# Modulation of a transformer block pair: matmul strips replaced by VectorE dot products over a transposed weight, and the first context-key product moved behind the branch products

## What is computed

```
mod     = silu(c)     @ w_mod + b_mod   -> shift1, scale1, gate1, shift2, scale2, gate2
mod_ctx = silu(c_ctx) @ w_mod + b_mod   -> shift1, scale1 (only these two are used)
h   = rmsnorm(x)   * (1 + scale1) + shift1          attention input of block 2
ctx = rmsnorm(ctx) * (1 + scale1_ctx) + shift1_ctx  its context keys and values
x   = x + gate1 * attention(h, [ctx, h])
h2  = rmsnorm(x) * (1 + scale2) + shift2            input of router and experts
x   = x + gate2 * experts(h2)
```

## Time and profile before

| | value |
|---|---|
| median of 3 runs | 1057.99 us (1057.42 to 1058.18) |
| span of the profiled execution | 1055.0 us |
| what lies around the span, median less span | 3.0 us |
| PE busy | 988.6 us, 94% |
| DVE busy | 525.0 us, 50% |
| ACT busy | 423.2 us, 40% |
| POOL busy | 154.5 us, 15% |
| DMA | 246.60 MB, mean 234 GB/s |

### The profile page before, as it was taken

The page is one execution under the profiler, slowest core; times in us unless marked ns, Lnnn a source line. Parts: engine busy times, 40 slices in busy tenths (PEclk is TensorE's granted clock), DMA queues, the critical chain, the costliest instruction groups (busy, mean ns, idle before and its releaser), DMA issues.

```text
span 1055.0 us, 13905 instructions
## 1 busy us (share of the span) xinstructions
PE 988.6 (94%) x5609; PEld 733.3 (70%) x5609; DVE 525.0 (50%) x703; ACT 423.2 (40%) x619; POOL 154.5 (15%) x97
## 2 busy tenths in 40 slices
PE   5999999888999999999999989999999999999992
PEld 5997888665998988988798856666776444344331
DVE  5656654783665445546607516777466222212224
ACT  4446844523454334435444434565232322222111
POOL 4001000000000000000097844455000000000000
PEclk9999999988999999999999999999997999999997
DMA  9745552439644764757354522325898899999981
GB/s 306 249 146 199 199 185 95 160 123 332 221 162 160 271 235 148 264 180 255 124 169 152 182 98 80 116 85 188 319 356 331 330 421 421 422 421 421 421 362 42
DMA packets 84675, 246.60 MB, mean 234 GB/s; under 512 B 4420, under 2 KB 8283, under 8 KB 72191
## 3 DMA queue, kind: packets, MB, share of 16 engines
q1 hardware_dynamic: 82224, 240.20, 60.9%
q0 software_dynamic: 1408, 4.00, 1.4%
q10 hardware_dynamic: 974, 1.45, 0.4%
HBM read 244.59 MB, written 1.05 MB: 233 GB/s over the span
## 4 chain that ended last, share of the span: by engine, by line
PE 83%; DVE 10%; ACT 2%; issue 2%; DMA 2%; POOL 1%; SPq 0%; DVEq 0%; POOLq 0%; ACTq 0%
PE gemm_ps L1268 10%; PE gemm_ps L774 8%; PE gemm_ps L776 8%; PE gemm_ps L775 8%; PE gemm_ps L778 7%; PE gemm_ps L780 7%; PE gemm_ps L779 7%; PE gemm_ps L1309 6%; PE gemm_ps L959 2%; PE mix_ps L774 2%; PE mix_ps L775 2%; PE mix_ps L776 2%; DVE w_lo L457 2%; PE mix_ps L1319 1%; PE mix_ps L1074 1%
## 5 line engine op out<-in xcount | busy, mean ns | idle before, releaser
L451 ACT ACTIVATE w_hi<-ring 128x1024 fp32r<-128x1024 f32 (+2 forms) x222 | 227.2, 1035 | 237.1 <-PE gemm_ps L780 95.0
L457 DVE TENSOR_TENSOR w_lo<-ring,w_hi 128x1024 fp32r<-128x1024 f32 (+2 forms) x174 | 203.7, 1187 | 164.2 <-ACT w_hi L451 163.4
L778 PE MATMUL gemm_ps<-acts,w_hi 128*128 128x256 f32 x640 | 184.9, 289 | 4.1 <-DVE acts L1851 2.8
L774 PE MATMUL gemm_ps<-w_hi,acts 128*128 128x512 f32 (+2 forms) x448 | 176.6, 394 | 8.0 <-DVE w_lo L457 7.1
L779 PE MATMUL gemm_ps<-acts,w_hi 128*128 128x256 f32 x640 | 181.8, 284 | 0.0
L780 PE MATMUL gemm_ps<-acts,w_lo 128*128 128x256 f32 x640 | 181.8, 284 | 0.0
L775 PE MATMUL gemm_ps<-w_lo,acts 128*128 128x512 f32 (+2 forms) x448 | 171.9, 384 | 0.0
L776 PE MATMUL gemm_ps<-w_hi,acts 128*128 128x512 f32 (+2 forms) x448 | 171.7, 383 | 0.0
L457 POOL TENSOR_TENSOR w_lo<-ring,w_hi 128x1024 fp32r<-128x1024 f32 x48 | 122.6, 2573 | 89.1 <-ACT w_hi L451 89.1
L778 PEld LDWEIGHTS gemm_ps<-acts,w_hi 128*128 128x128 f32 x640 | 123.5, 193 | 9.5 <-issue 6.2
L779 PEld LDWEIGHTS gemm_ps<-acts,w_hi 128*128 128x128 f32 x640 | 123.5, 193 | 1.3 <-issue 1.2
(11 more groups left out here) (367 smaller groups left out, 1317.3 us busy)
## 6 DMA issues: line engine op xcount, KB each, us to landing
ring<-in_w_in_dram SPq DMA_DIRECT2D x56, 1024.0 KB, 5.0
ring<-in_w_mod_dram SPq DMA_DIRECT2D x24, 1024.0 KB, 5.7
ring<-in_w_ffn_in_dram SPq DMA_DIRECT2D x20, 1024.0 KB, 5.1
late_ring<-in_w_exp_down_dram SPq DMA_DIRECT2D x20, 1024.0 KB, 16.8
late_ring<-in_w_exp_gate_dram SPq DMA_DIRECT2D x18, 1024.0 KB, 15.7
late_ring<-in_w_exp_up_dram SPq DMA_DIRECT2D x18, 1024.0 KB, 14.0
ring<-in_w_ffn_out_dram SPq DMA_DIRECT2D x11, 1024.0 KB, 9.2
ring<-in_w_exp_up_dram SPq DMA_DIRECT2D x9, 1024.0 KB, 17.3
```

The lines of the kernel that those rows point to most:

```text
L451: nc.scalar.activation(part(w_hi, u), raw_unit(u), ACT.Copy).then_inc(hi_made, 1)
L457: eng.tensor_tensor(part(w_lo, u), raw_unit(u), part(w_hi, u), ALU.subtract).then_inc(lo_made[unit["maker"]], 1)
L774: mm(dst, xh, wh, start=a_, stop=False, skip_group_check=True)
L778: mm(dst, wh, xh, start=a_, stop=False, skip_group_check=True)
```

## The change

The host hands over `w_mod` transposed (6144 x 1024), so that a feature's weights lie along a row. Each of 32 loads brings 256 features (1 MB, two rows of 1024 for each partition) through the same ring. DVE multiplies each row with SiLU of `c` or `c_ctx`, which lies on all partitions (`c_rows`, two DMAs on POOL's queue and two ACT operations), sums it and adds the bias, with one `tensor_tensor_reduce` for 128 features; `mod_dots(n)` does n loads. The context's parts come first and are read separately from those of `c`, so 32 MB of `w_mod` are loaded where it was 24 MB. The loads lie in the ring at 13 places among the gate chunks, 4 around `w_out`, and 15 in the feed-forward, none later. The gates' columns are multiplied into diagonals by POOL (`gate_diagonal`) and spread by one product with ones (`gate_spread`). All strips, turns and bias products of the modulation, and their copies on ACT, are gone.

The context rows are now scaled on ACT, turned in the middle of the branch products, and converted on ACT alone (`half_cols`) with DVE's subtraction (`half_low`) between the branch adds. On PE the first context-key chunk follows the branches directly, with the turn of the merged rows in its middle, then both halves of `w_out`, then the second context-key chunk. The merged rows are converted straight from PSUM in two halves (`high_cols`, `low_cols`). The sides of `acts` (0 and 1) are exchanged for the operands, and the slots of the expert weights are filled in another order: those in the ring as soon as their last piece is split.

```diff
+MODS = [("ctx", part, j) for part in (0, 1) for j in range(0, KT, 2)]
+MODS += [("c", part, j) for part in (0, 1, 3, 4) for j in range(0, KT, 2)]
+MODS += [("gate", part, j) for part in (2, 5) for j in range(0, KT, 2)]
+GATE_MODS = (1, 1, 2, 2, 2, 2, 2, 1)
+OUT1_MODS = (2, 2)
+FFN_GATE_MODS = 3
...
+    def features(kind, part, j):
+        if part in (3, 4):
+            own = w_mod[D * part + COL * (j // 4):D * part + COL * (j // 4 + 1), :].rearrange("(p k) n -> p k n", k=4)
+            return "mod", own[:, j % 4:j % 4 + 2, :]
+        return "mod", w_mod[D * part + P * j:D * part + P * (j + 2), :].rearrange("(k p) n -> p k n", p=P)
...
+    for i in range(8):
+        out.append(("gate", cols(w_in, GATE_RAW + COL * i)))
+        out += next_mods(GATE_MODS[i])
     wb = a["w_branch"][0].rearrange("n c d -> (n c) d")
     out += [("branch", cols(wb, COL * h)) for h in range(2)]
-    mod = [("mod_T", cols(w_mod, D * part + COL * h)) for part in (0, 1, 3, 4) for h in range(2)]
-    out1 = [("out1", cols(a["w_out"][0], COL * h)) for h in range(2)]
-    out += [out1[0], mod[0], mod[1], mod[2], mod[3], out1[1]]
-    out += [("kc", cols(w_in2, K_OFF + COL * i)) for i in range(2)]
+    out.append(("kc", cols(w_in2, K_OFF)))
+    for h in range(2):
+        out.append(("out1", cols(a["w_out"][0], COL * h)))
+        out += next_mods(OUT1_MODS[h])
+    out.append(("kc", cols(w_in2, K_OFF + COL)))
...
     for i in range(FFN_GROUPS):
         out.append(ffn("ffn_u", i))
+        out += next_mods(1)
         if i + 1 < FFN_GROUPS:
             out.append(ffn("ffn_g", i + 1))
+        if i < FFN_GATE_MODS:
+            out += next_mods(1)
         out.append(ffn("ffn_o", i))
-        if i < 4:
-            out.append(mod[i + 4])
+        out += next_mods(1)
+    assert not mods
     out += [("vc", cols(w_in2, V_OFF + COL * i)) for i in range(2)]
...
+            for slot in after_split:
+                last_here = [q for i, q in enumerate(pieces) if i % RING == slot - after_split[0]][-1]
+                for u in last_here["units"]:
+                    sp.wait_ge(lo_made[units[u]["maker"]], units[u]["lo"] + 1)
+                load_late(FIRST + slot)
+            assert [units[u]["split"] % UNITS for u in units_of[index["out2_b"][0]]] == [2, 3]
+            sp.wait_ge(*last_product(index["out2_b"][0]))
+            for slot in after_half:
+                load_late(FIRST + slot)
+            sp.wait_ge(*last_product(index["out2_b"][1]))
             for slot in after_out2:
...
+            def gate_diagonal(n):
+                if n == 0:
+                    pool.wait_ge(sem("scores"), HEADS2 * TT)
+                    pool.wait_ge(sem("mod_dots"), len(MODS))
+                else:
+                    p = spread_steps[n - 1]
+                    pool.wait_ge(made[p % 2], 2 * (p // 2) + 2)
+                own = gate_cols[:, n // 2, 4 * (n % 2):4 * (n % 2) + 4]
+                nc.gpsimd.tensor_tensor(DIAG, ident.unsqueeze(1).to_broadcast([P, 4, P]), own.unsqueeze(2).to_broadcast([P, 4, P]),
+                                        ALU.mult).then_inc(sem("diagonal"), 1)
...
+                if half == 1:
+                    turn("ctx", CTX)
...
+            def kc(c, after_unit=()):
+                p = step["kc1" if c else "kc0"]
                 pair_free_wait(pe, p)
-                strips(p, SILU_B, whole(index["mod_T"][c]), range(KT)).then_inc(made[p % 2], 1)
...
+            def turn_merged():
+                pe.wait_ge(cols_dve, 2 * TURN["ctx"] + 2)
+                turn("merged", XN)
+
+            cols_ready("ctx")
+            kc(0, after_unit=[lambda: None, turn_merged])
             cols_ready("merged")
-            out1(0, after_unit=[lambda: None, lambda: modulation_rows(1)])
-            modulation_cols(1)
-            turn("ctx", CTX)
-            modulation_rows(2)
-            modulation_rows(3)
...
+            def gate_spread(n):
+                p = spread_steps[n]
+                pair_free_wait(pe, p)
+                pe.wait_ge(sem("diagonal"), n + 1)
+                mm(bank(p, 1), ones, DIAG.rearrange("p k n -> p (k n)"), start=True, stop=True).then_inc(made[p % 2], 2)
...
+            def half_cols(name, r, full, half, scale, shift):
+                for k in range(4 * half, 4 * half + 4):
+                    if k % 2 == 0:
+                        act.wait_ge(turned, 4 * TURN[name] + k // 2 + 1)
+                    link(A(full[:, k, :], turned_to(name, k), ACT.Identity, scale=scale(k), bias=shift(k)))
+                A(place[:, r, 0, 4 * half:4 * half + 4, :], full[:, 4 * half:4 * half + 4, :], ACT.Copy).then_inc(cols_act, 1)
...
+            for t in range(TT):
+                j = 2 * NORM["ctx"] + t
+                act.wait_ge(sem("root_ready"), ctx_root + t)
+                A(CTX[:, t, :], CTX[:, t, :], ACT.Copy, scale=rs[:, j:j + 1]).then_inc(rows_ready, 1)
+            hi_up_to(units_of[index["branch"][1]][1])
             act.wait_ge(sem("mod_cols"), 1)
-            cols("ctx", 1, TF_C, scale=lambda k: modT[:, 1, k, 1:2], shift=lambda k: modT[:, 0, k, 1:2])
+            for half in range(2):
+                half_cols("ctx", 0, TF_C, half, lambda k: modT[:, 1, k, 1:2], lambda k: modT[:, 0, k, 1:2])
+                hi_up_to(units_of[index["branch"][1]][2 + half])
+            hi_up_to(units_of[index["kc"][0]][2])
+            high_cols("merged", 1, 0)
+            high_cols("merged", 1, 1)
...
+            def half_low(name, r, full, half):
+                own = slice(4 * half, 4 * half + 4)
+                dve.wait_ge(cols_act, HIGH_BEFORE[name] + 1 + half)
+                V_.tensor_tensor(place[:, r, 1, own, :], full[:, own, :], place[:, r, 0, own, :], ALU.subtract).then_inc(cols_dve, 1)
...
+            def mod_dots(n):
+
+                for i in range(mods_done[0], mods_done[0] + n):
+                    kind, part, j0 = MODS[i]
+                    piece = units[units_of[index["mod"][i]][0]]["piece"]
+                    own = (0, 1, None, 2, 3, None)[part]
+                    if i == 0:
+                        dve.wait_ge(sem("c_rows"), 2)
+                        dve.wait_ge(sem("small"), 16 * 12)
+                    landed_wait(dve, piece)
+                    for t in range(2):
+                        j = j0 + t
+                        w = raw(piece)[:, t, :]
+                        bias = late_feats[:, part - 3, j:j + 1] if part in (3, 4) else feat("b_mod_2", KT * part + j)
+                        dst = gate_cols[:, part // 3, j:j + 1] if kind == "gate" else modT[:, own, j, 1:2] if kind == "ctx" else modT[:, own, j, 0:1]
+                        ins = V_.tensor_tensor_reduce(w, w, c_rows[:, 1 if kind == "ctx" else 0, :], 1.0, bias, ALU.mult, ALU.add, dst)
+                    ins.then_inc(sem("mod_dots"), 1)
+                    if kind != "gate" and part in (1, 4) and j0 == KT - 2:
+                        dve.wait_ge(sem("mod_dots"), i + 1)
+                        g = late_feats[:, 2, :] if part == 4 else feats("norm1_g_2", 0, 8)
+                        v = modT[:, own, :, 1 if kind == "ctx" else 0]
+                        V_.scalar_tensor_tensor(v, v, 1.0, g, ALU.add, ALU.mult).then_inc(sem("mod_cols"), 1)
+                mods_done[0] += n
...
             V_.tensor_copy(NLF.rearrange("p t h n -> p (t h) n"), fs[:, 0:8].unsqueeze(2).to_broadcast([P, 8, P])).then_inc(sem("fox_f"), 1)
+            mod_dots(2)
+            lo_to("gate", 3, 3)
+            mod_dots(2)
             lo_to("gate", 4, 3)
+            mod_dots(2)
             dve.wait_ge(sem("stick_c"), 1)
...
+            lo_to("gate", 5, 3)
+            mod_dots(2)
             lo_to("gate", 6, 3)
+            mod_dots(2)
...
+            lo_to("kc", 0, 3)
+            low_cols("merged", 1, 0, 1.0)
+            low_cols("merged", 1, 1, 1.0)
...
+            lo_to("out1", 0, 3)
+            mod_dots(2)
+            lo_to("out1", 1, 1)
             add_out1(0)
-            modulation(1)
-            modulation(2)
-            modulation(3)
...
+                if c >= 1:
+                    lo_to("ffn_o", c - 1, -1)
+                    mod_dots(1)
+                lo_to("ffn_u", c, -1)
+                mod_dots(1)
...
+                if c < FFN_GATE_MODS:
+                    lo_to("ffn_g", c + 1, -1)
+                    mod_dots(1)
+            lo_to("ffn_o", FFN_GROUPS - 1, -1)
+            mod_dots(1)
...
+    arrays["in_w_mod_2_dram"] = _np.ascontiguousarray(inputs["w_mod_2"][0].T)
```

304 lines of the change are left out of this document (103 added, 201 removed).

## The result

The changed kernel takes 1034.28 us, the median of 4 runs (1033.89 to 1036.62), against 1058.09 for the kernel before in the same call. The ratio is 0.9776 with a 95% interval of 0.9756 to 0.9796. The forecast was 1031.0 with a range of 1020 to 1048. The profiled execution has a span of 1032.4 us, so 22.6 us less than before: most of the time is there, but the table shows that it came in part from other places than the sum said.

The account below looks back on a forecast made before the run. PE was taken to bound the kernel, with 83% of the span on its chain of waits. Terms -14.4 - 9.5 - 1.9 - 12.5 + 7.3 + 3.6 = -27.4 took 1058 to 1031 us, range 1020 to 1048.

Parts of the forecast that it names:

- The likeliest case: Whole kernel: the forecast of 1031 us itself, its own range 1024 to 1040, chance 0.55.
- The dot: New DVE product with sum: 1.28 + 0.15 = 1.44 us each, between bounds of 1.22 and 2.7.
- FFN, -14.4: Feed-forward: four modulation chunks leave PE, 4 x 3.6 us; the dots fit into DVE's slack.
- From the branches to the turn of x2, -12.5: Branches to turn of `x2`: 95.2 us become 82.7, with the first context-key chunk starting at +34.7.
- Gate chunks, +7.3: Gate stage: dots ahead of gate chunk 3 make its `w_lo` unit late, 125.6 against 118.3 us.
- The start, 0: Start to first product: no change forecast, 0 us.
- End of the FFN, +3.6: End of the FFN: an add 1.2 us later behind dots, and 2.4 for the context columns behind `mod_dots(1)`.
- Output products, -9.5 and -1.9: Output products to logits: strips, bias products and idle go, -9.5 us; logits to gather, 9.0 us instead of 10.9, -1.9.
- Experts, 0: Expert stage: paced by PE and DMA alike, moves rigidly, no gain and no loss.
- Double dots: Rival: a dot takes 2.7 us, adding 44 us over gate chunks, `w_out`, FFN and its end; 1075 us, chance 0.12.
- DVE's order costs twice: Rival: waits of DVE's order cost twice the count, with lower clock in the gaps; 1046 us, chance 0.17.
- the waits do not appear: Rival: smaller gap at gate chunk 3, first context-key chunk at +30, `x2` in time; 1020 us, chance 0.12.

Follow-up runs that it names:

- a_gate: Changed kernel with VectorE's order around gate chunk 3 altered: dots put between the `w_lo` units instead of four ahead of them; 1033.78 us, ratio 0.9748.
- a_spread: Changed kernel with five modulation loads moved from the gate stage to the FFN, one load per gate chunk, 20 in the FFN; 1029.40 us, ratio 0.9731.

## Why the prediction was right, point by point

**The whole.** 1031.0 was forecast, 1034.3 measured, the sign and eight tenths of the size right (22.6 of 27.4 us in the traces). The likeliest case was the one that came, within its own range. That the sum is only 4.8 us off is partly luck: the stages' errors add up to some 20 us without their signs, and 5.3 more than forecast won ahead of the turn of `x2` stand against 3.0 at the start and 4.5 behind the heads. The mechanism held where most of the time is (strips and turns off PE in the FFN, the chunk over turn and conversion).

**The dot.** The value taken, 1.44 us, was 1.20: the record is as long as L2433's, but each dot starts 0.08 us before the record of the one ahead of it ends, and the second row adds nothing. The upper bound of 2.7 is out. The rule of the Trainium skill that was weighed ("Vector Engine (DVE) Microarchitecture Reference", "Points that are easy to get wrong": halved throughput with two SBUF sources that are not bf16) names the form `S2S2D2_STT`, and the dot is recorded as a custom operation, so this run does not test it; two float32 rows from SBUF, with a sum, took 1280 ns for 1024 elements. The prediction's reading, that L2433 speaks against the rule, was too quick, since it compared with a subtraction that has two sources as well. Against an operation with one source,

```profile
L1805 DVE TENSOR_SCALAR arena<-x_sb,st 128x1024 f32<-128x1024 f32 x6 | 4.5, 755 | 4.1 <-POOL st L660 4.1
```

in the kernel before, L2433 takes 1.7 times as long. Against the same form with one source in PSUM it does not (128x512: 683 ns at L2212, 751 with both in SBUF at L2175). Which comparison the rule means, it does not say. The dot's price in the sum was off for another reason: the 0.15 us counted for the second row don't show in a row of dots.

**FFN, -14.4.** Measured -15.5. Where the step "4 x 3.6" was short: PE also lost a little at each change between products and strips or turns (behind the strips of 341.77 the first product takes 0.32 us of the chain, the next 0.12). The dots are hidden in full; even doubled they cost nothing there. That contradicts the 8 us which the rival counted for the FFN.

**From the branches to the turn of x2, -12.5.** Measured -17.8, and the turn at the lower clock gives 1.7 back, which was not counted. The terms that failed are the start of the first context-key chunk (+34.7 forecast; it started at 236.51, 31.5 behind 205.0) and the two waits of 1.3 and 2.2 us at `w_out`, where only 0.3 us shows. Of the first term it was the 4.5 us for ScalarE's new work that was too large: VectorE's adds end at 242.2, 37.2 behind 205.0, where 31.6 + 3.7 + 4.5 = 39.8 was put in, so that 1.9 of the 4.5 are left. The wait for the rows of `x2` was 2.9 where 3.7 stood. Undoing the move costs 6.6 us, so the part of the argument that the chunk covers turn and conversion is shown.

**Gate chunks, +7.3.** Measured +8.5, at the place that was named, ended by the named unit. But the size agrees by luck: chunk 3 comes 5.9 us late instead of 7.3 (127.31, against 118.35 and the 3.04 lost at the start), mostly since four dots take 4.8 and not 5.8 us, and 2.6 us are slower matmuls (13.5 against 10.9; the 11.18 in the expectation of `a_gate` is in no row), which the prediction mentioned but left without a price. The prediction did not have what `a_gate` shows: in another order on VectorE the wait came back one chunk later, since the ring is released in that order too.

**The start, 0.** Measured +3.0: a term that the sum doesn't have. The change takes two 4 KB loads from SP's queue, ahead of the first megabyte, and putting them back returned 2.45 of the 3.04 us. The prediction looked at SP's queue for the ring, not for the first microseconds.

**End of the FFN, +3.6.** Measured +4.7, but not in the terms forecast. PE idles 3.12 us between the two halves of the context turn, where it was 0.85 (+2.3 against the +1.2 forecast), and not behind dots. The chain there:

```profile
468.84 5.14 DMA ring<-in_w_in_dram
...
474.00 1.06 ACT w_hi L473
...
475.09 0.04 DVE w_lo L479
...
476.23 0.69 DVE arena L2085
```

The last hidden product (L2085) stands behind a `w_lo` unit whose ring load landed at 473.98, and without any dots the wait is as long (3.2). Which load of the changed ring order makes it late was not tried. The 2.4 us for the context columns show as a wait of 0.40 for their conversion (L1824) and as 0.4 us more ahead of a later `w_lo` unit (2.32 against 1.95). The rest lies in matmuls at the lower clock level, which the sum left out: behind the first gap the half turn took 1.94 instead of 1.06 us.

**Output products, -9.5 and -1.9.** Measured -6.0 and -0.9. The step that failed is "what PE sheds there is on the path": the first strips and the idle ahead of them, 2.8 us, covered four PSUM reads by VectorE, and a wait of 2.2 us remains (shown by reading in the other order). Two more waits, 0.88 and 0.80, stand where strips stood or where a ring load is late. For the second the chain names a load of 12.5 us; that the expert loads ahead of it in SP's queue make it so slow was not tried. Behind the logits PE now waits 3.5 us for VectorE's selection, which is what the forecast said would be late next; the interval came out at 10.1 instead of 9.0 us.

**Experts, 0.** Measured -1.3 from the gather to the end. No run says whether that is the new order of the slots.

**Rivals.** Double dots were priced at +44 with 1.26 us more per dot; measured +32 for the same 1.26, which is 23 in the gate stage (22 forecast), 9 at `w_out` (10), nothing in the FFN (8), 2.5 at its end (4). A dot of 2.46 us gives 1066; the rival's 2.7 us and 1075 were not run, but it would have been slower than before all the same. Of the case "DVE's order costs twice", one trait came true, the lower clock in the gaps; of the case "the waits do not appear", the early start of the context-key chunk.

## What to carry to other kernels

Work that goes to an engine with a low busy share is free only where that engine's queue has slack ahead of what the bound engine waits for; look stage by stage, and spread it by the least slack, not evenly over the program. When an in-order engine also releases a buffer ring, putting its extra work earlier delays its products and putting it later can delay the loads: here only less work per turn of the ring removed the wait. To tell an engine's work from the loads that feed it, take the work out and leave the loads: such runs overturned a theory about the gate stage and show that a wait at the end of the FFN is not one for dots. Before counting a removed instruction as a gain, look at what the other engines finish while it runs.

## What the runs showed of the hardware

The VectorE dot with its sum is recorded as 1280 ns for 128x1024 float32, and dots start 1.20 us apart in a row. In the kernel before, an operation of that shape with one source takes 755 ns. With two loads of 4 KB gone from ahead of a 1 MB load, which is issued 0.7 us earlier, the first product starts 3.0 us later, and putting them back returns 2.45 us. In the changed kernel PE came back at the lower clock level after gaps of 2.86, 3.12 and 4.05 us: the sixteen matmuls of a turn took 3.59 us instead of 1.75. It is not so after each such gap: with fewer loads in the gate stage (`a_spread`) the same half turn of the context rows came after a gap of 2.84 us and took 1.06 us, at the full level.
